# The prologue of a two-layer decoder trunk, rebuilt: order of loads, halves of the input, and what PSUM feeds

## The reference

```python
def _rms_norm(x, g):
    xf = x.astype(jnp.float32)
    y = xf * lax.rsqrt(jnp.mean(xf * xf, axis=-1, keepdims=True) + EPS)
    return (y * g.astype(jnp.float32)).astype(x.dtype)

def _swiglu(x, wi, wo):
    a, b = jnp.split(x @ wi, 2, axis=-1)
    return (jax.nn.silu(a) * b) @ wo

h = x
for l in range(DEPTH):
    h = h + 0.5 * _swiglu(_rms_norm(h, norm_ffn1[l]), ffn1_wi[l], ffn1_wo[l])
    n = _rms_norm(h, norm_mix[l])
    ...
```

## Time and profile before

| what | value |
| --- | --- |
| median of 3 runs | 2720.15 us |
| lowest and highest run | 2715.23 and 2720.67 us |
| span of the profiled execution | 2716.9 us |
| its own time beside the span | not recorded; the median run is 3.25 us above the span |
| PE busy | 2664.1 us, 98% of the span |
| DVE, ACT, POOL busy | 49%, 41%, 45% |
| first transpose, first product | 9.00 and 18.51 us |

### The profile page before, as it was taken

The page is one execution under the profiler, slowest core; times in us unless marked ns, Lnnn a source line. Parts: engine busy times, 40 slices in busy tenths (PEclk is TensorE's granted clock), DMA queues, the critical chain, the costliest instruction groups (busy, mean ns, idle before and its releaser), DMA issues.

```text
span 2716.9 us, 36975 instructions
## 1 busy us (share of the span) xinstructions
PE 2664.1 (98%) x13132; PEld 2137.3 (79%) x13132; DVE 1326.2 (49%) x1834; ACT 1100.5 (41%) x1664; POOL 1230.2 (45%) x616
## 2 busy tenths in 40 slices
PE   8999999989999999999999999999899999999999
PEld 6888888766678868888888888887667788788887
DVE  5221258786535554252541212777865364543533
ACT  5322242446644454222342223434476445542222
POOL 4444456672235424444444434567522354344443
PEclk9999999999999999999999999999999999999999
DMA  4334433222224313333333353432122342233332
GB/s 133 95 99 113 115 98 87 70 55 55 55 78 117 109 47 107 94 99 95 91 95 101 93 132 92 111 79 68 49 55 63 86 124 85 62 101 101 93 100 78
DMA packets 493612, 243.41 MB, mean 90 GB/s; under 512 B 49468, under 2 KB 491174, under 8 KB 493478
## 3 DMA queue, kind: packets, MB, share of 16 engines
q1 hardware_dynamic: 492960, 241.49, 32.0%
q10 hardware_dynamic: 518, 0.13, 0.0%
HBM read 239.46 MB, written 2.10 MB: 89 GB/s over the span
## 4 chain that ended last, share of the span: by engine, by line
PE 65%; issue 16%; POOL 8%; DVE 5%; ACT 3%; POOLq 2%; DVEq 1%; ACTq 0%; DMA 0%; SPq 0%
PE pg L636 20%; PE pg L639 19%; PE pg L642 19%; POOL wL L585 7%; PE pA L706 2%; DVE convb L1740 1%; PE pA L911 1%; PE pA L858 1%; POOLq L612 1%; POOLq L614 1%; DVE prob L1902 0%; POOL wsn L610 0%; ACT prob L1156 0%; ACT wH L1156 0%; ACT hH L1156 0%
## 5 line engine op out<-in xcount | busy, mean ns | idle before, releaser
L585 POOL TENSOR_TENSOR wL<-raw,wH 128x1024 fp32r<-128x1024 f32 (+1 forms) x472 | 1084.9, 2300 | 1453.2 <-ACT wH L1156 1449.4
L636 PE MATMUL pg<-gxH,wH 128*128 128x512 f32 (+1 forms) x2448 | 960.6, 392 | 3.6 <-DVE gxL L1601 3.1
L642 PE MATMUL pg<-gxH,wL 128*128 128x512 f32 (+1 forms) x2448 | 948.7, 388 | 0.0
L639 PE MATMUL pg<-gxL,wH 128*128 128x512 f32 (+1 forms) x2448 | 944.1, 386 | 0.0
L1156 ACT ACTIVATE wH<-raw 128x1024 fp32r<-128x1024 f32 (+1 forms) x472 | 475.8, 1009 | 834.3 <-PE pg L642 673.5
L636 PEld LDWEIGHTS pg<-gxH,wH 128*128 128x128 f32 x2448 | 461.0, 188 | 110.7 <-issue 18.4
L639 PEld LDWEIGHTS pg<-gxL,wH 128*128 128x128 f32 x2448 | 461.2, 188 | 93.6 <-issue 7.1
L642 PEld LDWEIGHTS pg<-gxH,wL 128*128 128x128 f32 x2448 | 461.0, 188 | 93.2 <-issue 3.9
L642 PE MATMUL pg<-hH,wL 128*128 128x512 f32 x992 | 392.7, 396 | 0.0
L636 PE MATMUL pg<-hH,wH 128*128 128x512 f32 x992 | 390.5, 394 | 1.5 <-DVE hL L1657 1.5
L639 PE MATMUL pg<-hL,wH 128*128 128x512 f32 x992 | 390.6, 394 | 0.0
(11 more groups left out here) (234 smaller groups left out, 2208.8 us busy)
## 6 DMA issues: line engine op xcount, KB each, us to landing
raw<-in_ffn_wi SPq DMA_DIRECT2D x352, 256.0 KB, 3.1
raw<-in_w_in SPq DMA_DIRECT2D x200, 256.0 KB, 3.3
raw<-in_ffn_wo SPq DMA_DIRECT2D x128, 256.0 KB, 3.0
raw<-in_ffn_wo SPq DMA_DIRECT2D x64, 192.0 KB, 2.6
raw<-in_xkv SPq DMA_DIRECT2D x32, 256.0 KB, 3.0
raw<-in_w_out SPq DMA_DIRECT2D x32, 256.0 KB, 3.0
raw<-in_sgu_out SPq DMA_DIRECT2D x32, 128.0 KB, 2.2
raw<-in_conv_out SPq DMA_DIRECT2D x32, 128.0 KB, 2.2
```

The lines of the kernel that those rows point to most:

```text
L585: pool.tensor_tensor(wL[:, s % 4, 0:n, :], raw[:, s % 2, 0:n, :], wH[:, s % 4, 0:n, :].bitcast(F32), ALU.subtract)\
L636: mm(o, wH[:, s, k, :], rh(k), start=(k == 0), stop=False)
L639: mm(o, wH[:, s, k, :], rl(k), start=False, stop=False)
L642: last = mm(o, wL[:, s, k, :], rh(k), start=False, stop=(k == kt - 1))
```

## The change

- The SP queue now loads weight unit 0 first, then x in two column halves (eight DMAs of 256 KB, pro_ld[0] for the first half and pro_ld[1] for the second), then unit 1, then 18 small parameter loads (`param_loads`), then units 2 and 3. ACT issues only the load of the first norm's gain.
- PE transposes that gain alone first (gain_tr), DVE copies it into par (gain_in). The eight tiles of x are transposed into eight banks, four of pg and four of pA (`first_bank`).
- ACT makes gxH straight from the PSUM bank, and copies the bank to xT too. The split of unit 1 stands between tiles 3 and 4. DVE makes gxL from the PSUM bank, tile by tile, and frees the first four banks one by one.
- The other parameters are transposed on PE after unit 2 (par_tr). DVE copies them after rstd is made and raises par_in. ACT waits for par_in after the root, before it enters the feed-forward block.

```diff
 # sync
-            for a in range(TT):
-                sp.dma_start(xnat[:, a, :], x[0, a * P:(a + 1) * P, :]).then_inc(pro_ld, 16)
...
+                    if l == 0 and u == 0:
+                        unit(l, 0, 0, cols_of(wi, 0))
+                        for hf in range(2):
+                            for a in range(TT):
+                                cols = slice(hf * T, (hf + 1) * T)
+                                sp.dma_start(xnat[:, a, cols], x[0, a * P:(a + 1) * P, cols])\
+                                    .then_inc(pro_ld[hf], 16)
+                        unit(l, 1, 0, cols_of(wi, F))
+                        param_loads()
+                        unit(l, 2, 0, cols_of(wi, P))
+                        unit(l, 3, 0, cols_of(wi, F + P))
+                        first = 1
 # tensor, in ffn, after unit c of the first four
+                            if c == 2 and l == 0 and f == 0:
+                                pe.wait_ge(pro_par, 16 * (10 + 8))
+                                for j in range(L):
+                                    last = turn(pT[:, j * P:j * P + NP_ROWS],
+                                                ctab[0:NP_ROWS, j, :], NP_ROWS)
+                                last.then_inc(par_tr, 1)
 # tensor, prologue
-            pe.wait_ge(pro_ld, 16 * TT)
+            pe.wait_ge(pro_gain, 16)
+            turn(pT[:, 0:KD], ctab[0:KD, 0, :], KD).then_inc(gain_tr, 1)
             for k in range(KD):
-                if k >= 4:
-                    pe.wait_ge(pro_cp, k - 4 + 1)
+                if k % 4 == 0:
+                    pe.wait_ge(pro_ld[k // 4], 16 * TT)
+                if k == 6:
+                    pe.wait_ge(gain_in, 1)
                 for a in range(TT):
-                    last = turn(pg[:, k % 4, a * P:(a + 1) * P], xnat[:, a, k * P:(k + 1) * P])
+                    last = turn(first_bank(k)[:, a * P:(a + 1) * P],
+                                xnat[:, a, k * P:(k + 1) * P])
                 last.then_inc(pro_tr, 1)
...
 # scalar
+            act.dma_start(ctab[G_F1:G_F1 + KD, 0:L, :],
+                          norm_ffn1.rearrange("l (a b) -> a l b", b=P)).then_inc(pro_gain, 16)
             act.wait_ge(consts, 1)
             split(0, 0)
-            split(0, 1)
-            act.wait_ge(par_in, 1)
-            norm(0, 0, G_F1, gx_tile, None)
+            act.wait_ge(gain_in, 1)
+            for k in range(KD):
+                if k == 4:
+                    split(0, 1)
+                act.wait_ge(pro_tr, k + 1)
+                copy(gxH[:, k, :], first_bank(k), scale=col(G_F1 + k)).then_inc(gx_h, 1)
+                copy(xT[:, k, :], first_bank(k)).then_inc(pro_cp, 1)
+            act.drain()
+            for k in range(KD):
+                act.wait_ge(sq_used, risen(sq_used, 0, k - 1))
+                act.activation(sq[:, k % 2, :], xT[:, k, :], ACT.Square).then_inc(sq_done, 1)
             for l in range(L):
                 split(l, 2)
                 made[0] = 3
                 root(l, 0, rstd, 1.0 / D)
+                if l == 0:
+                    act.wait_ge(par_in, 1)
                 ffn(l, 0, (1, G_MIX, gx_tile))
 # vector
+            dve.wait_ge(gain_tr, 1)
+            dve.tensor_copy(par[:, G_F1:G_F1 + KD], pT[:, 0:KD])
+            dve.drain().then_inc(gain_in, 1)
+            dve.sem_inc(evac, risen(evac, 0, 0) - 4)
             for k in range(KD):
-                dve.wait_ge(pro_tr, k + 1 if k < 5 else k + 2)
-                if k == 5:
-                    dve.tensor_copy(par[:, 0:NP_ROWS], pT[:, 0:NP_ROWS]).then_inc(par_in, 1)
-                dve.tensor_copy(xT[:, k, :], pg[:, k % 4, :]).then_inc(pro_cp, 1)
-            dve.drain().then_inc(evac, risen(evac, 0, 0))
+                dve.wait_ge(pro_cp, k + 1)
+                STT(gxL[:, k, :], first_bank(k), col(G_F1 + k), gxH[:, k, :].bitcast(F32),
+                    ALU.mult, ALU.subtract).then_inc(gx_l, 1)
+                if k < 4:
+                    dve.drain().then_inc(evac, 1)
...
             for l in range(L):
                 root_of(l, 0, rstd)
+                if l == 0:
+                    dve.wait_ge(par_tr, 1)
+                    dve.tensor_copy(par[:, KD:NP_ROWS], pT[:, KD:NP_ROWS]).then_inc(par_in, 1)
+                    for j in range(1, L):
+                        dve.tensor_copy(pall[:, j, :], pT[:, j * P:j * P + NP_ROWS])
+                    dve.drain()
+                    gains()
+                    dve.drain()
                 ffn(l, 0, 0, (1, gx_high, gx_low, G_MIX))
```

More of the change, by code:

```diff
@@ L352, in trunk @@
         consts = ctx.enter_context(nc.semaphore("consts"))
-        pro_ld = ctx.enter_context(nc.semaphore("pro_ld"))
+        pro_ld = [ctx.enter_context(nc.semaphore(f"pro_ld{i}")) for i in range(2)]
+        pro_gain = ctx.enter_context(nc.semaphore("pro_gain"))
+        gain_tr = ctx.enter_context(nc.semaphore("gain_tr"))
+        gain_in = ctx.enter_context(nc.semaphore("gain_in"))
+        par_tr = ctx.enter_context(nc.semaphore("par_tr"))
         pro_par = ctx.enter_context(nc.semaphore("pro_par"))
@@ L369, in trunk, with first_bank @@
         pconst = ctx.enter_context(nc.semaphore("pconst"))
+        def first_bank(k):
+            return pg[:, k, :] if k < 4 else pA[:, k - 4, :]
         block = ctx.enter_context(nc.Block())
@@ L407, in at_col, with param_loads @@
                 return src
+            def param_loads():
+                for g, at in ((norm_mix, G_MIX), (norm_xattn, G_X),
+                              (mem_norm, G_MEM), (norm_ffn2, G_F2), (conv_b, P_CB),
+                              (conv_ln_g, P_LG), (conv_ln_b, P_LB), (sgu_norm, P_SG),
+                              (xq_norm, P_XQ), (xk_norm, P_XK)):
+                    n = g.shape[1] // P
+                    sp.dma_start(ctab[at:at + n, 0:L, :], g.rearrange("l (a b) -> a l b", b=P))\
+                        .then_inc(pro_par, 16)
+                for half in range(2):
+                    cols = slice(half * DH, (half + 1) * DH)
+                    for g, at in ((nsa_q_norm.rearrange("l (a c) -> a l c", a=1), P_NQ),
+                                  (nsa_k_norm.rearrange("l a c -> a l c"), P_NK),
+                                  (cmp_pe.rearrange("l i a c -> i a l c")[0], P_PE),
+                                  (cmp_pe.rearrange("l i a c -> i a l c")[1], P_PE + CMP_LEN)):
+                        n = g.shape[0]
+                        sp.dma_start(ctab[at:at + n, 0:L, cols], g).then_inc(pro_par, 16)
             def small_loads(l):
@@ L431, in ffn @@
                         before_last(l)
-                    with sp.Fori(0, n // 2) as i:
+                    first = 0
+                    if l == 0 and u == 0:
[10 more added lines that the diff above has]
+                        first = 1
+                    with sp.Fori(first, n // 2) as i:
                         for c in range(4):
@@ L1187, in high @@
                         act.wait_ge(evac, risen(evac, l, u0 + k - 3))
-                    elif u0 is None:
-                        act.wait_ge(pro_cp, k + 1)
                     else:
@@ L1196, in square @@
                     act.activation(sq[:, k % 2, :], xT[:, k, :], ACT.Square).then_inc(sq_done, 1)
-                if u0 is None:
-                    for k in range(KD):
-                        high(k)
                 for k in range(KD):
[L1202 to L1208, removed]
+                    if u0 == U_XO:
+                        if k == 6:
+                            ahead(l, U_XO + 3)
+                    else:
+                        ahead(l, u0 + k + lead)
+                    high(k)
                     if not late:
@@ L1611, in add @@
                         TTt(sacc[:, :], sacc[:, :], sq[:, k % 2, :], ALU.add).then_inc(sq_used, 1)
[L1612 to L1626, removed]
+                for k in range(KD):
+                    update(k)
+                    if k >= 1:
+                        low(k - 1)
+                    if k >= 2 and not late:
+                        add(k - 2)
+                low(KD - 1)
+                for k in range(0 if late else KD - 2, KD):
+                    add(k)
                 stat_given(None)
@@ L1676, in _ @@
             dve.wait_ge(consts, 1)
+            dve.wait_ge(gain_tr, 1)
+            dve.tensor_copy(par[:, G_F1:G_F1 + KD], pT[:, 0:KD])
+            dve.drain().then_inc(gain_in, 1)
+            dve.sem_inc(evac, risen(evac, 0, 0) - 4)
             for k in range(KD):
-                dve.wait_ge(pro_tr, k + 1 if k < 5 else k + 2)
-                if k == 5:
-                    dve.tensor_copy(par[:, 0:NP_ROWS], pT[:, 0:NP_ROWS]).then_inc(par_in, 1)
-                dve.tensor_copy(xT[:, k, :], pg[:, k % 4, :]).then_inc(pro_cp, 1)
-            dve.drain().then_inc(evac, risen(evac, 0, 0))
+                dve.wait_ge(pro_cp, k + 1)
[3 more added lines that the diff above has]
+                    dve.drain().then_inc(evac, 1)
+            for k in range(KD):
+                dve.drain()
```

(6 more changed lines are left out.)

5 lines of the change are left out of this document (removed).

## The result

| | kernel before | changed kernel |
| --- | --- | --- |
| median, 16 runs each | 2719.35 us | 2725.44 us |
| lowest and highest run | 2714.81, 2723.02 | 2722.32, 2726.63 |
| ratio to before | | 1.0021, 95% interval 1.0014 to 1.0028 |
| span of the profiled execution | 2716.9 us | 2721.9 us |
| its own time | not recorded | 2723.66 us |

The kernel became slower: 0.21% is 5.7 us, with an interval of 3.8 to 7.6. The profiled executions are 5.0 us apart. One run of experiment e1 took 10852 us and one of e2 4095 us: all ratios leave them out, while the two medians in the table of experiments count them (without them they are 2716.66 and 2719.5).

A forecast was written before the change was run, and what follows sets the result against it. TensorE, busy 98% of the span, was taken as the bound, so the start of unit 3 or 4 counts. Front -3.4, wait +5.4, clock +1.5 gave +3.5 us: 2723.7 us, range 2718.5 to 2727.5.

The forecast's parts named there:

- rivals 3 and 4: Unit 3 wholly at the lower clock, chance 0.12; front gains nothing, unit 2 at 31.5, chance 0.12; each +7, 2727.
- The wait for par_in: Before unit 3: ACT's split waits until unit 2 is through; unit 2 to unit 3 takes 11.6 us instead of 6.2.
- The clock: Behind PE's idle time before unit 3: the lower clock level costs 1.5 us, bounds 0 and 3.4.
- The front: Prologue up to unit 2: new load order and ACT copies start unit 2 at 28.0 against 31.41, gaining 3.4 us.
- The sum: Whole kernel: -3.4 (front) + 5.4 (unit 2 to unit 3) + 1.5 (clock) = +3.5 us; chance 0.55.
- The small loads on SP: Prologue: 18 parameter loads issued from about 5.8 to 13.4, unit 2 landing before 18; six us of cover, cost nothing.
- The rule on transposes: Input transposes: the skill's rule would give 0.43 us each, unit 2 near 32; the forecast used the row's 0.215 us.
- Later stages hidden: After unit 3: unit 4's split and unit 5's load move about 2 us while PE comes 3.5 us later; hidden.
- Rival 5: Before unit 3: par_in wait already met, unit 3 at 34.6, gain 3.0 us, 2717.1; chance 0.07.
- rival 4: Prologue: late x, unoverlapped ACT copies or slow transposes; unit 2 at 31.5, in all +7, 2727; chance 0.12.

The follow-up runs named there:

- e1: Changed kernel with only ACT's wait for par_in moved from before unit 3's split to ahead of the second norm; 2717.09 us, ratio 0.9991 to the kernel before.
- e2: Changed kernel, wait kept, with PE's two parameter transposes moved ahead of unit 2; 2720.00 us, ratio 0.9999 to the kernel before.
- e3: Kernel before plus the wait, with the transposes behind unit 2 and DVE copies it needs, old loads and front; 2727.64 us, ratio 1.0029.
- e9: Changed kernel, its wait kept, with x loaded in four row blocks behind unit 0 instead of column halves; 2727.03 us, ratio 1.0028 to the kernel before.
- e4: e1 with SP's first loads reordered: first half of x, unit 0, second half of x, unit 1; 2718.84 us, ratio 0.9994 to the kernel before.
- e7: e1 with x loaded in four row blocks behind unit 0 instead of column halves; 2718.97 us, ratio 0.9996 to the kernel before.
- e8: The changed kernel run again without edits; 2725.07 us, ratio 1.0020 to the kernel before.
- e6: e1 with the parameters' work after the first chunk's column units and unit 2's split ahead of the fourth square; 2717.80 us, ratio 0.9993.

## Why the prediction was right, and where its sizes were off

The forecast was 2723.7 with +3.5 us and "within 0.2%" as the likeliest; measured were 2725.44 and +5.7 us, inside the range and just beyond the bound of 0.2%. The interval, 0.14 to 0.28%, has that bound in it, so on which side of it the kernel lies is not settled. The time alone could not have chosen the forecast: 2725.44 is as near to the 2727 of rivals 3 and 4 as to 2723.7. The profile chooses: unit 2 starts at 29.89 and not at 31.5, and nine products of unit 3 ran at the lower level and not all 24. The mechanism is the one it named, and it is shown by e1 (taken out of the changed kernel), e2 (shortened) and e3 (put into the kernel before). Step by step:

- **The wait for par_in: right in place and size.** Predicted 11.6 us from unit 2 to unit 3, measured 11.40, 11.39 (e3) and 11.38 (e9). The table load stands behind the wait (36.47 to 37.75), as the sum had it. Split to low took 1.13 us (37.76 to 38.89), the low 2.35.
- **The clock: right.** Predicted 1.5 us. The first nine spacings in unit 3 take 4.01 us (41.29 to 45.30) against 2.19 in the kernel before (37.60 to 39.79), 1.8 us lost. (The stretch that the 1.5 us were taken from, has PE at work for 3.1 us at the lower level, from 18.51 to 21.57, and not for 2.7.)
- **The front: the term that was mis-sized.** "In the new order unit 0 lands at 4.4, the first half of x at 4.4 + 2 x 1.47 = 7.35". Unit 0 was there at 5.46, where ACT's table load starts, 1.1 late, and the first transpose came at 9.76, 4.3 behind it instead of 2.95. The range had 8.8 as its latest, too early as well. ACT's start moved from 8.5 to 10.98, the first sum from 19.3 to 21.44, unit 2 from 28.0 to 29.89. The front gained 1.5 us instead of 3.4. The step that was off carried the flow of x in 4 KB rows over to a queue of 512-byte and 2 KB pieces; why that queue was slower was not separated. Some of it is scatter: in e1, with the same loads, the first transpose came at 8.73. The copies' cost (1.1 a tile, measured 1.06) and the chain behind them were right: 9.6 us from the first gxH to the end of the last xT copy (forecast 9.9), and 8.45 from the first sum to unit 2 (forecast 8.7).
- **The sum**: -1.5 + 5.2 + 1.8 = +5.5, against 5.0 between the spans and 5.7 by the ratio. The mis-sized front is nearly the whole of the difference to the +3.5 that was forecast.
- **The small loads on SP: right.** They were issued from 7.42 to 16.02, later than the 5.8 to 13.4 of the forecast. Unit 2's loads went out at 16.06 and landed by 19.8, not before 18; the split that needs them came at 26.37, so about 6 us of cover were left. e1, with the loads in place, is no slower than the kernel before (0.9991, 0.9982 to 1.0000).
- **The rule on transposes: the row was misread, and the sum did not hang on it.** The prediction took 0.215 us per transpose for the upper level. It is the lower one. In the changed kernel the starts are 0.213 us apart up to 14.72 and 0.109 apart from 14.85 on, and the first record of the granted clock in its trace is at 14.73; in the kernel before the change comes at 14.74. The first sixteen took 3.67 us, the other sixteen 2.65. So the 0.43 us that the prediction set against the row, as what the slow level would cost, doubled a number that was the slow one already. The Trainium skill, "TensorE: Matmul & The Clock Gate", Part 4 (PE-mode transpose), says that the full clock does not engage for transposes. The trace agrees for the first 23 of them and not for the rest: the clock rose while PE had done nothing but transposes. The forecast used the measured spacing and not its level, so its sum stays.
- **Later stages hidden: right.** The waits of PE from 0 to 200 us hold nothing behind unit 3.

Rival 5, that the wait costs nothing, is close to what e1 makes of the kernel: 2717.09 measured, 2717.1 written for it. That the two agree to the hundredth is luck: e1's unit 2 started at 28.85 and not at 28.0, its transposes took less than was written, and runs of one kernel scatter by several us. Rivals 3 and 4 did not happen in full; the front's shortfall of 1.9 us is about half of rival 4's.

## What to carry to other kernels

When work is moved off the start of a kernel, follow who waits for its result and what that engine had still to do for the bottleneck engine. A wait placed one statement too early put a split, a table load and a low part behind a whole unit of matmuls, and cost more than the rebuilt prologue gained. Read an engine's pace against another stretch of the same work before you say at which clock it ran. A transfer that moves up the queue pushes the next one back, so a front with two inputs starts with the later of them.

## What the runs showed of the hardware that was not expected

**The flow into SBUF dips.** Windows of 1 us of the changed kernel; the last number is GB/s. The loads of x were issued from 1.88 on.

```profile
5.00:6.00 1.00, 0.27 (x1) 0.18 (x1) 0.00 (x0) 0.54 (x1) 0.62 (x3) 1.00 0.92 294
...
6.00:7.00 1.00, 0.00 (x0) 0.00 (x0) 0.17 (x1) 0.99 (x2) 0.00 (x0) 1.00 0.76 217
...
7.00:8.00 1.00, 0.00 (x0) 0.00 (x0) 0.00 (x0) 0.81 (x1) 0.11 (x1) 1.00 0.81 246
...
8.00:9.00 1.00, 0.00 (x0) 0.00 (x0) 0.00 (x0) 0.00 (x0) 1.00 (x1) 1.00 0.97 301
```

Between 5 and 8 us the queues moved 217 to 294 GB/s, where the kernel before, with x in 4 KB rows first, moved 363 to 418 (and 323 to 404 in e3, with the same loads). Every order with weights or halves ahead had such a dip (e4: 215 to 232 between 4 and 7; e7: 112 and 205 between 4 and 6). The cause, piece size or the change from one size to another, was not separated.

**PE starts at the lower level, and the windows do not say so.** A row over the transposes of the kernel before (shortest, median and longest, in ns), and two windows of e1:

```profile
L706 PE MATMUL pg<-ident,big x32: 272/421/445, 9.0 to 15.4; 128*128 128x128 f32 x32
...
10.00:11.00 1.00, 1.00 (x7) 1.00 (x6) 0.00 (x0) 1.00 (x2) 0.07 (x1) 1.00 1.06 375
...
12.00:13.00 1.00, 1.00 (x11) 1.00 (x11) 0.75 (x1) 1.00 (x3) 0.00 (x0) 1.00 0.52 127
```

In 11 of the 12 traces the spacing halves at the first record, which lies between 11.6 and 18.6 us. In e4 the first record is at 16.23: all 32 transposes kept 0.213 us, and the first products came at 15.18, 15.75 and 16.18, and from 16.44 on 0.23 us apart.

**The clock's fall after a hole is not a matter of the hole's length alone.** It fell in the hole of 5.4 us (changed kernel, e3, e8, e9), in the one of 2.8 us ahead of unit 0 (kernel before) and behind one of 1.91 us (e6), and not behind 2.62 us (e2) nor behind 3.56 us ahead of unit 0 (e3). Later in the kernel it differs between two executions of the same kernel: from 2320 to 2330 us the changed kernel was granted 1.00 in its first profile and 0.66 in the one of e8. The time of a run goes with its mean granted clock: runs of the kernel before with 0.997 took 2711.6 to 2717.1 us, those with 0.994 took 2718.9 to 2722.5. So single runs of one kernel lie up to 11 us apart, and differences of 1 us between versions stay open here.
